# A hybrid attention and state-space layer with product-key experts: the compression in four column groups, its pieces between the halves of the projections

## What is computed

```
c = split_columns(rmsnorm(x) @ w_in)
o_ret  = retention(ret_q, ret_k, ret_v, ret_g)          # decayed linear attention
o_moba = moba(rope(moba_q), rope(moba_k), moba_v)       # at 256 tokens: causal attention
o_ssm  = mamba2(z, conv(xbc), dt, ...)                  # chunked state space, one chunk of 256
o_nsa  = gate0 * o_cmp + gate1 * o_slc + gate2 * o_win
mixed  = concat(o_ret, o_moba, o_ssm, o_nsa) @ w_out
```

```
def compress(t, pe, w1, w2):
    blocks = (t[:, win_idx] + pe).reshape(b, nc, 32 * 64)
    return gelu(blocks @ w1) @ w2           # w1: 2048 x 256, w2: 256 x 64
```

## Time and profile before

| | us |
|---|---|
| median of 3 runs | 2022.0 |
| lowest, highest | 2021.11, 2022.18 |
| the profiled execution | 2021.42 |
| its span, first to last instruction | 2019.6 |
| TensorE busy | 1986.5 |
| VectorE, ScalarE, GpSimd busy | 1199.5, 991.7, 1244.8 |

### The profile page before, as it was taken

One profiled execution on the slowest core, in us unless ns is written; L12 is line 12 of the kernel. 1 busy time (PEld: TensorE's weight loads), 2 busy tenths in 40 slices (PEclk: granted clock), 3 DMA queues, 4 the chain that ended last, 5 costly groups with the idle time before them and its releaser, 6 DMA issues.

```text
span 2019.6 us, 41560 instructions
## 1 busy us (share of the span) xinstructions
PE 1986.5 (98%) x14222; PEld 1820.7 (90%) x14222; DVE 1199.5 (59%) x2732; ACT 991.7 (49%) x1557; POOL 1244.8 (62%) x622
## 2 busy tenths in 40 slices
PE   9999999999999999999999999999999999999998
PEld 9798999999999888888897889999999998888886
DVE  4464298249999444444454624971699994444444
ACT  5545444654443544545555454456444445454544
POOL 6345688876666555555463466888766665555553
PEclk9999999999999999999999999999999999999999
DMA  6423555554444555555544245555444445555553
GB/s 214 165 95 127 185 180 186 177 167 146 146 146 146 182 192 196 190 196 190 189 143 163 80 150 179 186 175 185 161 146 146 146 140 193 196 190 196 189 195 135
DMA packets 93243, 338.46 MB, mean 168 GB/s; under 512 B 10352, under 2 KB 10736, under 8 KB 93168
## 3 DMA queue, kind: packets, MB, share of 16 engines
q1 hardware_dynamic: 93168, 337.53, 50.1%
HBM read 336.44 MB, written 1.05 MB: 167 GB/s over the span
## 4 chain that ended last, share of the span: by engine, by line
PE 96%; DVE 2%; ACT 1%; issue 0%; DMA 0%; DVEq 0%; SPq 0%; ACTq 0%
PE PS L920 34%; PE PS L857 12%; PE PS L862 12%; PE PS L858 12%; PE PS L556 6%; PE PS L871 4%; PE PS L540 2%; PE PS L545 2%; PE PS L541 2%; PE PS L782 2%; PE PS L664 1%; PE PS L522 1%; PE PS L593 1%; PE PS L625 0%; PE PS L627 0%; PE PS L628 0%
## 5 line engine op out<-in xcount | busy, mean ns | idle before, releaser
L459 POOL TENSOR_TENSOR WL<-ring,WH 128x1024 fp32r<-128x1024 f32 x360 | 870.9, 2422 | 435.1 <-ACT WH L1154 229.3
L1154 ACT CAST WH<-ring 128x1024 fp32r<-128x1024 f32 x512 | 537.9, 1051 | 689.2 <-PE PS L920 327.0
L489 POOL TENSOR_TENSOR HL<-G,HH 128x256 fp32r<-128x256 f32 x256 | 372.7, 1456 | 324.1 <-ACT HH L1256 323.9
L1775 DVE TENSOR_TENSOR WL<-ring,WH 128x1024 fp32r<-128x1024 f32 x248 | 303.8, 1225 | 370.9 <-ACT WH L1154 370.9
L857 PE MATMUL PS<-HH,WH 128*128 128x256 f32 x2048 | 512.2, 288 | 0.0
L858 PE MATMUL PS<-HL,WH 128*128 128x256 f32 x2048 | 501.3, 283 | 0.0
L858 PEld LDWEIGHTS PS<-HL,WH 128*128 128x128 f32 x2048 | 392.2, 192 | 0.0
L857 PEld LDWEIGHTS PS<-HH,WH 128*128 128x128 f32 x2048 | 391.2, 191 | 0.0
L920 PE MATMUL PS<-WH,HH 128*128 128x512 f32 x1024 | 315.5, 389 | 3.0 <-issue 3.0
L920 PE MATMUL PS<-WH,HL 128*128 128x512 f32 x1024 | 315.2, 389 | 0.0
L1724 DVE SCALAR_TENSOR_TENSOR OH<-IOB,slotT,PS 128x384 bf16<-128x384 bf16 x512 | 308.6, 603 | 0.0
(11 more groups left out here) (247 smaller groups left out, 2151.6 us busy)
## 6 DMA issues: line engine op xcount, KB each, us to landing
ring<-stream SPq DMA_DIRECT2D x636, 512.0 KB, 3.3
X<-x_t SPq DMA_DIRECT2D x4, 256.0 KB, 3.8
out_t<-X SPq DMA_DIRECT2D x2, 512.0 KB, 2.7
CN<-consts SPq DMA_DIRECT2D x1, 843.5 KB, 9.6
WF<-last SPq DMA_DIRECT2D x1, 512.0 KB, 10.1
PR<-params SPq DMA_DIRECT2D x2, 239.0 KB, 4.0
CN<-consts SPq DMA_DIRECT2D x1, 64.0 KB, 3.8
```

The source lines that it names most:

```text
L459: nc.gpsimd.tensor_tensor(WL[:, b, :], ring[:, slot, :], WH[:, b, :].bitcast(F32), ALU.subtract).then_inc(done, 1)
L489: nc.gpsimd.tensor_tensor(GL[:, s, :], G[:, tile, :], GH[:, s, :].bitcast(F32), ALU.subtract).then_inc(L.gl_ready, 1)
L1154: nc.scalar.copy(WH[:, b, :], ring[:, slot, :]).then_inc(L.hi_ready, 1)
L1775: V.tensor_tensor(WL[:, s % 2, :], ring[:, (U0 + s) % SLOTS, :], WH[:, s % 2, :].bitcast(F32), ALU.subtract).then_inc(L.vlo_ready, 1)
```

## The change

1. **The stream.** Two functions, slot_of and slot_of_w1, give the slots 14 to 29 anew: 11's first half, piece 0 of w1, 11's second half, piece 1, and so on to 14's second half and piece 7. So 14's first half is slot 26, and 15's first half stays slot 30.
2. **The compression.** A piece is one step, compress(m). Its four matmuls write to the partitions 32j to 32j + 31 of bank 7 (tile_position (0, 32j)), each over all four pieces of a key or value. BL is padded from 15 to 32 columns with zeros (a memset on GpSimd). The four groups are summed when the hidden values are turned: in place of four transposes, four matmuls with a 128 x 15 constant (sum4). The Gelu comes after that sum, in the copies into HV.
3. **TensorE's order.** Projections 11 to 17 are cut into halves, with work between them; the decays (acr, now in bank 6), the cumulative sums and the state space values move from behind 13 to 16 forward to 11 to 14; the compressed scores, kcvc and the values of window and selection move back.
4. **ScalarE's and VectorE's orders** are rebuilt to match; casts are taken out of take(n) and placed singly.

The core of the diff:

```
+def slot_of(u, k):
+    if 11 <= u <= 14:
+        return 2 * W1 + 4 * (u - 11) + 2 * k
+    return 2 * u + k
+def slot_of_w1(m):
+    return 2 * W1 + 2 * m + 1
...
+                    def compress(m):
+                        i, k = m // 4, m % 4
+                        if k == 0:
+                            pe.wait_ge(padded, 2 * layer + 1)
+                            pe.wait_ge(L.blocks_ready, i + 1)
+                        w = piece(slot_of_w1(m)).rearrange("p (j m) -> p j m", j=CHUNKS // 4)
+                        for j in range(CHUNKS // 4):
+                            mm = nc.tensor.matmul(bank[7][32 * j:32 * j + 32, i * 256:(i + 1) * 256],
+                                                  BL[:, i, CHUNKS // 4 * k + j, :], w[:, j, :],
+                                                  start=(k == 0), stop=(k == 3), tile_position=(0, 32 * j))
+                        mm.then_inc(L.piece_done, 1)
...
+                    project(11, (0,))
+                    pe.wait_ge(L.tr_evac, 4)
+                    two_scores(TK_WIN, 0)
+                    compress(0)
...
+                    acr(1)
+                    project(13, (0,))
+                    compress(4)
+                    turn_group(SC4[0], 0)
+                    project(13, (1,))
+                    compress(5)
+                    project(14, (0,))
+                    turn_group(SC4[1], 1)
+                    compress(6)
+                    pe.wait_ge(L.seg_ready, 4)
+                    pe.wait_ge(L.ps_ready, 2)
+                    values(lambda h: SEG[:, h, :], lambda h: [XDT[:, t, h * HD:(h + 1) * HD] for t in range(TT)])
+                    project(14, (1,))
+                    compress(7)
...
                     for i in range(4):
-                        mm = nc.tensor.transpose(bank[7][:, 16 * i:16 * i + NCMP],
-                                                 HID[0:NCMP, i // 2, i % 2 * P:(i % 2 + 1) * P], ident[0:NCMP, 0:NCMP])
+                        mm = nc.tensor.matmul(bank[7][:, 16 * i:16 * i + NCMP],
+                                              HID[:, i // 2, i % 2 * P:(i % 2 + 1) * P], cn("sum4"), start=True, stop=True)
...
                     exps(0, SC4[0])
...
+                    upper(2 * PROJ.index(13))
+                    take(12, next_too=False)
+                    for q in (1, 2):
+                        upper(2 * PROJ.index(13) + q)
+                    probabilities(PT[0])
+                    act.wait_ge(L.seg_ready, 4)
+                    nc.scalar.activation(SEG[:, :, :], SEG[:, :, :], ACT.Exp).then_inc(seg_exp, 1)
+                    exps(1, SC4[1])
+                    take(13, next_too=False)
+                    for q in (1, 2):
+                        upper(2 * PROJ.index(14) + q)
+                    probabilities(PT[1])
+                    take(14, next_too=False)
```

More of the change, by code:

```diff
@@ L546, in by_column @@
                             mm.then_inc(L.piece_done, 1)
[L548 to L572, removed]
@@ L582, in project @@
                         else:
-                            by_token(n, j % 2)
+                            for k in halves:
+                                by_token(n, j % 2, k)
                     sets = [0]
@@ L655, in _ @@
                         scores(XC[:, 2 + g, :], XC[:, 4 + g, :], False)
[L658 to L670, removed]
@@ new lines, in two_scores, with acr @@
+                    def two_scores(key, h):
+                        for i in (h, h + 1):
+                            scores(half(TQ_NSA + i // 2, i), half(key, i), True)
+                    dta_t = dta.rearrange("p (t h) -> p t h", t=TT)
+                    tri = cn("tri")
+                    def acr(pair):
+                        for i in range(2):
+                            h = 2 * pair + i
+                            nc.tensor.matmul(bank[6][:, i * SEQ:(i + 1) * SEQ], DA[:, 0, h, :], tri[:, 0:SEQ],
+                                             start=True, stop=False)
+                            mm = nc.tensor.matmul(bank[6][:, i * SEQ + P:(i + 1) * SEQ], DA[:, 1, h, :],
+                                                  tri[:, SEQ:SEQ + P], start=False, stop=True)
+                        mm.then_inc(L.acr_done, 1)
@@ L677, in _ @@
                     mm.then_inc(hid_tr, 1)
-                    turn_group(SC4[0], 0)
-                    project(12)
+                    pe.wait_ge(L.roped, 3)
+                    turn(columns(MOBA_Q))
+                    turn(columns(MOBA_K))
+                    project(15, (0,))
                     pe.wait_ge(L.hid_ready, 3)
@@ L687, in _ @@
                     mm.then_inc(kcvc_done, 1)
[L688 to L705, removed]
@@ L707, in acr @@
-                    def acr(pair):
-                        for i in range(2):
-                            h = 2 * pair + i
-                            nc.tensor.matmul(bank[7][:, i * SEQ:(i + 1) * SEQ], DA[:, 0, h, :], tri[:, 0:SEQ],
-                                             start=True, stop=False)
-                            mm = nc.tensor.matmul(bank[7][:, i * SEQ + P:(i + 1) * SEQ], DA[:, 1, h, :],
-                                                  tri[:, SEQ:SEQ + P], start=False, stop=True)
-                        mm.then_inc(L.acr_done, 1)
@@ L1079, in _ @@
                     taken(T[:, TQ_NSA:TQ_NSA + 2, :]).then_inc(L.tr_evac, 1)
+                    for q in (1, 2):
+                        upper(2 * PROJ.index(11) + q)
+                    take(11, next_too=False)
+                    upper(2 * PROJ.index(12) + 1)
                     exps(0, SC4[0])
[L1081 to L1085 removed]
```

299 lines of the change are left out of this document (173 added, 126 removed).

## The result

The changed kernel takes 2044.1 us (median of 4 runs, 2043.1 to 2045.2) against 2022.0 for the kernel before; the ratio is 1.0109, 95% interval 1.0095 to 1.0123. I had forecast 2022.8 within 2017 to 2033, so it came out 21 us later than forecast and outside the range. The profiled execution took 2043.83 us, with a span of 2042.0.

What follows compares the result with a forecast made beforehand. TensorE's own work was taken to bound the kernel, busy 1986.5 of 2019.6 us. Savings and new costs summed to +0.4 us a layer, +0.8 in all, giving 2022.8 us, with an 8-in-10 range of 2017 to 2033.

Steps and rivals of the forecast that it cites:

- Compression: Compression pieces on four column groups: 0.65 us a piece, 14.4 down to 5.2 us, a gain of 9.2 us a layer.
- Rival C: Compression's four groups don't run side by side: 1.3 us a piece gives 2032 us, 1.94 gives 2041; chance 0.18.
- Interruptions: Projections 11 to 17 cut in halves: seven more interruptions at 0.18 us each, +1.2 us a layer.
- the hidden values' turn: Four full fp32 matmuls summing the groups replace four transposes: 0.95 us instead of 0.34, +0.6 us.
- The two new waits: TensorE waits at turn_group 0 and 1 for copies behind casts: 3.9 and 4.5 us, +7.0 us a layer.
- The first pair of scores: First state-space scores wait for VectorE to empty banks 4 and 5, holding TensorE 2.0 us, not 1.22: +0.8 a layer.
- its WL of 2.38 us has room behind every ScalarE cast here: GpSimd's WL subtraction fits behind each rebuilt cast, so zeroing the padding on GpSimd was given no cost.
- The sum of work and waits: Per layer: -9.2 + 1.2 + 0.6 + 0.8 + 7.0 = +0.4 us, +0.8 over two layers.
- The clock: At TensorE's new waits, clock falls were left out of the forecast: waits exceed the 3.4 us idle stretch only by little.
- A: The forecast itself: column groups side by side and both new waits present, 2018 to 2026 us; chance 0.47.
- rival B: TensorE's clock falls in the new waits: one to four falls at 2.4 us each, 2025 to 2032 us; chance 0.20.
- 6 us at 0.6 of the pace: Price of one clock fall, read from TensorE's matmuls per microsecond at the kernel's start: 2.4 us lost.

Runs made afterwards that it cites:

- e6_one_group: e5_evac_early with the four matmuls of each compression piece on one 32-column group, one after the other: 2025.4 us, ratio 1.0019.
- e8_bank6_first: e5_evac_early with VectorE's addition that empties bank 6 moved ahead of the rotation of projection 13: 2005.1 us, ratio 0.9915.
- e11_pool_later: e9_gate_back with GpSimd's WL subtraction for projection 11's second half held until VectorE's copies of the state-space scores are done: 2006.3 us, ratio 0.9922.
- e4_spins: The changed kernel with its three waits a layer filled by matmuls that nothing reads: 2024.8 us, ratio 1.0015.
- e9_gate_back: e8_bank6_first with VectorE's gate operations back ahead of its copies of the state-space scores: 2015.4 us, ratio 0.9972.
- e5_evac_early: e3_both with ScalarE's four copies of turn_group 1 moved ahead of the evacuation of projection 13 and two casts: 2017.1 us, ratio 0.9970.
- e3_both: The changed kernel with ScalarE's turn_group copies ahead of the casts of slots 26 and 30, and VectorE's score copies ahead of its gate operations: 2009.1 us, ratio 0.9936.
- e10_groups_gs: The kernel before with the column groups alone, plus VectorE's copies of the state-space scores ahead of its gate operations: 2022.9 us, ratio 1.0003.
- e1_copies_first: The changed kernel with ScalarE's copies that empty turn_group 0 and 1 ahead of the casts of slots 26 and 30: 2019.3 us, ratio 0.9988.

## Why the forecast was wrong, step by step

**Compression, right.** 0.57 us a piece at the full clock where 0.65 was taken; 14.4 - 8 x 0.57 = 9.8 us a layer gained instead of 9.2. Rival C falls by the same row: the groups run side by side, and e6_one_group shows what it is like when they don't. The Trainium skill ("TensorE: Matmul & The Clock Gate", Part 3) has matmuls start and end in program order; as the earlier trace rows did, the record of the piece at 101.34 speaks against it for the two passes of an fp32 matmul: four records start within 0.02 us, the other four 0.24 us later, so the first passes of all four groups go ahead of any second pass.

**Interruptions and the hidden values' turn, right.** In e8_bank6_first the stage takes 85.58 us, 9.2 less than in the kernel before. 9.8 were gained on the pieces and 0.75 at turn_group 1 (1.08 to 0.33), so some 1.4 us are left for both; 1.8 were taken.

**The two new waits, right.** 3.67 + 4.36 for 3.9 + 4.5, by the chain that was written down.

**The first pair of scores, wrong in size and cause.** It was taken as 0.8 us a layer, on the ground that VectorE's copies come 3.0 us behind the same point as before. It waited 2.59. The step that failed is "its WL of 2.38 us has room behind every ScalarE cast here". The change moved ScalarE's cast of projection 11's second half, and so GpSimd's WL, forward, and the forecast looked only for whether WL was in time, not for who stands beside it: the WL came to lie on VectorE's gate operation, and the copies behind that came 2.3 us late (e11_pool_later).

**The sum of work and waits.** With 1.8 more for that pair, 0.4 less for the waits, 0.6 less for the pieces and 0.4 less for the interruptions, the forecast's +0.4 us a layer becomes +0.8. The stages of e4_spins, which has the waits without the clock's falls in them, are 0.9 and 0.7 us longer than in the kernel before. So this sum held, 2022.8 against the 2024.8 of that run, though in part because its errors cancel.

**The clock, the step that failed.** The forecast itself, A, put the clock at nothing: that all four waits are longer than the idle stretch of the earlier trace rows was set aside since "they are so by little". The fall was rival B, at 0.20, priced at 2.4 us a fall and one to four falls. There were six falls, since the 2.6 us waits bring one too, and e4_spins prices them at 19.2 us, 3.2 each. The price was wrong because it was read from the start of the kernel, as 6 us at 0.6 of the pace. Those two rows have a granted clock of 1.00 both, so they show no fall, and their 7 and 11 records count some that only reach into the microsecond: by their starts there are 4 or 5 a microsecond from 1 to 7 us and 9 after that. The rows of the changed kernel show 3.4 to 10.2 us at half the pace with TensorE busy. The chance was wrong because one row, a fall 3.4 us after the end, was read as the idle time that a fall needs. That row showed one case, and bounded nothing from below. The Trainium skill's page "TensorE: Matmul & The Clock Gate" (Part 1) says that the clock opens again only after sustained work, and the rows agree in that it doesn't come back with the work: TensorE is busy 9.93 us of the ten from 110 to 120 and the granted clock is 0.51.

With B at the measured size the sum is 2022.8 + 2 x 0.4 + 19.2 = 2042.8; the runs gave 2044.1. The range ended at 2033 because B's worst case, four falls, was priced at 9.6 us.

## What to carry to other kernels

Before adding a wait of 2 us or more to a TensorE that has been busy all along, ask what the clock does behind it: by the stages, each such wait cost 1.6 to 4.9 us more than its own length here (1.6 and 3.2 in e9_gate_back, 20.2 for the changed kernel's six, 4.8 and 4.9 in e5_evac_early against e8_bank6_first), a little under half the length of the fall. Of a slowdown of 22 us, 19 came back with all the waits left in place, their idle time filled with matmuls that nothing reads. Look for it in the granted clock and in the records started per microsecond, since the busy share stays at 100%. When an early cast is moved forward, follow what it releases on the other engines, and read what runs beside it there; and when the last long wait of a stage is removed, run again: the move that removed the last one from e3_both made another in e5_evac_early, and only e8_bank6_first was rid of both.

## What the hardware showed that was not expected

- In the profiled executions, every one of the 23 waits of 2.1 us or more in this stage had a fall to 1.2 GHz in it or behind it (2.1 us in e10_groups_gs, 2.2 in e5_evac_early, 2.6 in the changed kernel, e1_copies_first and e9_gate_back). At 1.4 to 1.7 us it was uneven: none behind the two of e1_copies_first; in e3_both a fall behind 1.52 us and none behind 1.69; and behind the 1.67 us wait at the first output product's second part 8 times in the 26 layers profiled, none of two in the kernel before and two of two in e8_bank6_first. So in this range the length of a wait doesn't decide alone. A kernel with such waits can also spread widely from run to run (e5_evac_early 2010 to 2019 in ten runs); it need not (the changed kernel, with six falls, 2043.1 to 2045.2 in four).
- Operations of VectorE that read only SBUF stood still beside a GpSimd subtraction: 2.33 instead of 0.17 us for 128x24, 2.61 instead of 0.42 for 128x256. Its copies out of PSUM, beside the same subtraction (61.08 to 63.53) in e3_both, kept their pace, two in 1.01 us, and only the gate operation behind them stood still again:

```profile
61.22 1.01 DVE L1558 COPY G<-PS 128x384 f32<-128x384 f32 x2
62.16 1.41 DVE L1561 TENSOR_SCALAR G<-G 128x24 f32<-128x24 f32 x1
```

  The Trainium skill's page "SBUF — State Buffer" ("SBUF: two separate sides") describes a port pair that the two engines share as an exclusive lock for a whole instruction; the rows agree, down to an operation of 24 columns waiting for one of 1024: it ends at 64.05, the subtraction at 64.02.
- Four fp32 matmuls on four column groups, two passes each, take 0.57 us, and 1.84 on one group: a factor of 3.2 for four.
